# Up projection of the second block's first feed-forward by seven half products instead of eight, inner features in four portions

## What is computed

```python
def conv_ffn(h, w_up, w_conv, b_conv, w_down):
    u = dwconv_centred(h @ w_up, w_conv, b_conv)
    g, v = jnp.split(u, 2, axis=-1)
    return (jax.nn.silu(g) * v) @ w_down
```

## Time and profile before

| | |
|---|---|
| median of 3 runs | 2653.69 us (2653.25 to 2664.85) |
| profiled execution, span | 2649.1 us |
| TensorE busy | 2552.1 us |
| VectorE busy | 1718.7 us |
| ScalarE busy | 1056.5 us |
| GpSimd busy | 24.3 us |

### The profile page before, as it was taken

How to read it: one execution, slowest core, us unless ns; L and a number is a source line. 1 busy time by engine, 2 the same in 40 slices (tenths; PEclk the granted TensorE clock), 3 DMA queues, 4 the chain that set the end, 5 groups by cost and what they waited for, 6 DMA issues and landing times.

```text
span 2649.1 us, 32136 instructions
## 1 busy us (share of the span) xinstructions
PE 2552.1 (96%) x13096; PEld 2130.9 (80%) x13096; DVE 1718.7 (65%) x2364; ACT 1056.5 (40%) x1455; POOL 24.3 (1%) x31
## 2 busy tenths in 40 slices
PE   7998999999999999999989999999999999999998
PEld 6887788888778888777768888888888787788887
DVE  6886798887688877768534655235534686663563
ACT  4546442233454245443442433123324564442342
POOL 0000000000100000000000000000000000000000
PEclk9999999999899999999999999999999999999999
DMA  8432388654145666211102122211211111233232
GB/s 287 168 120 75 99 291 299 214 187 143 53 135 192 207 197 222 84 61 47 62 9 64 49 64 65 71 56 64 73 63 56 56 45 44 80 97 103 96 97 87
DMA packets 90658, 296.69 MB, mean 112 GB/s; under 512 B 9216, under 2 KB 23168, under 8 KB 90256
## 3 DMA queue, kind: packets, MB, share of 16 engines
q1 hardware_dynamic: 90512, 294.64, 34.1%
HBM read 289.88 MB, written 2.10 MB: 110 GB/s over the span
## 4 chain that ended last, share of the span: by engine, by line
PE 85%; DVE 9%; ACT 3%; issue 2%; DMA 1%; SPq 0%; DVEq 0%; ACTq 0%
PE ps L372 69%; PE ps L400 3%; PE ps L3534 1%; PE ps L3209 1%; PE ps L974 1%; PE ps L3177 1%; DVE gatt L1003 1%; DMA spare<-in_ada_w 1%; PE ps L3190 1%; PE ps L2556 1%; DVE w_lo L353 1%; PE ps L590 1%; PE ps L1981 1%; ACT w_hi L345 0%; DVE spare L504 0%
## 5 line engine op out<-in xcount | busy, mean ns | idle before, releaser
L372 PE MATMUL ps<-h_hi,w_hi 128*128 128x512 f32 (+1 forms) x2344 | 784.4, 371 | 9.4 <-DVE w_lo L353 6.4
L372 PE MATMUL ps<-h_lo,w_hi 128*128 128x512 f32 (+1 forms) x2344 | 775.2, 367 | 0.0
L372 PE MATMUL ps<-h_hi,w_lo 128*128 128x512 f32 (+1 forms) x2344 | 774.9, 367 | 0.0
L353 DVE TENSOR_TENSOR w_lo<-w_raw,w_hi 128x1024 fp32r<-128x1024 f32 (+2 forms) x318 | 412.3, 1297 | 429.4 <-ACT w_hi L345 428.4
L345 ACT ACTIVATE w_hi<-w_raw 128x1024 fp32r<-128x1024 f32 (+2 forms) x318 | 355.2, 1117 | 737.2 <-PE ps L372 686.1
L372 PEld LDWEIGHTS ps<-h_hi,w_hi 128*128 128x128 f32 x2344 | 440.6, 189 | 90.6 <-DVE w_lo L353 11.0
L372 PEld LDWEIGHTS ps<-h_hi,w_lo 128*128 128x128 f32 x2344 | 442.4, 189 | 73.9
L372 PEld LDWEIGHTS ps<-h_lo,w_hi 128*128 128x128 f32 x2344 | 442.6, 189 | 72.9 <-issue 1.4
L372 PE MATMUL ps<-g_hi,w_hi 128*128 128x512 f32 (+1 forms) x880 | 295.7, 369 | 0.8 <-DVE w_lo L353 0.8
L372 PE MATMUL ps<-g_hi,w_lo 128*128 128x512 f32 (+1 forms) x880 | 294.8, 368 | 0.0
L372 PE MATMUL ps<-g_lo,w_hi 128*128 128x512 f32 (+1 forms) x880 | 294.8, 368 | 0.0
(11 more groups left out here) (460 smaller groups left out, 2705.9 us busy)
## 6 DMA issues: line engine op xcount, KB each, us to landing
...
```

The source lines that it names most:

```text
L353: dve.tensor_tensor(low, raw_weights(k, g), high.bitcast(F32), ALU.subtract).then_inc(*k.tick("w_lo", g))
L372: last = pe.matmul(k.ps[:, product_bank(g, bank) if place is None else place, 0:tn], a[:, c, :], b[:, c, t0:t0 + tn], start=c == 0 and n = ...
```

## The change

The up projection of a pair of tiles (u and v of group j, called A11 A12 over A21 A22 with the halves of the 1024 inputs as columns) times the input (B11 B12 over B21 B22: input halves as rows, token halves 0..383 and 384..767 as columns) is eight half products of 4 slices by 384 tokens. From the third group on the kernel forms it by Winograd's variant of Strassen's seven, m = 0 to 6 in the order of `SEVEN`: A11.B11, S1.T1, S2.T2, A12.B21, S3.T3, S4.B22, A22.T4. The two first groups stay as they were (`PLAIN`).

- GpSimd makes the T sums from the whole input (for even slices it first adds `h_hi` and `h_lo` to the whole value, `pool_whole`), in place, 4 sums of 384 columns for each of 4 slices (`pool_turned`), and for each group the four weight sums S1 to S4, 512 columns each (`pool_weight_sums`). Both inputs of all these lie in SBUF. The T sums are then split by ScalarE and VectorE; T1's parts replace a half of `h_hi` and `h_lo`, so they wait for the last plain tile's product.
- A weight operand is 512 columns; each of the seven is split by itself ("split 0" to "split 6") into a ring of three buffers.
- TensorE adds products up in three banks a group: m = 0, 2, 4 and 6 in the first one, 1 and 5 in the second, 3 in the third. ScalarE copies out the intermediate states (`first_kept`, `second_kept`, `fifth_kept`, `last_kept`) before the next product of the bank, and VectorE adds in place of a copy where two terms meet ("eleven" after m = 3, "twenty_two" after m = 4, "twelve" after m = 5). m = 2 waits for `first_kept`, 4 for `second_kept`, 5 for `fifth_kept` and 6 for `twenty_two`.
- Taps and centre now read the joined values from SBUF (`source7`), not from PSUM. The taps of group j run in the time of group j+1, between its splits.
- The 22 groups go in four portions of 6, 6, 6 and 4, each followed by 8 down tiles of 6, 6, 6 or 4 slices, every one added to `x`. Of the first two down tiles of a portion the last slice is held back behind the other slices of both.
- SyncE loads four pieces of 256 KB per group (`sp_quads`), into places inside the weight buffers, instead of two tiles of 512 KB.

```diff
     run("out2", "out2", 0, KD)
-    ffn(1, 0)
+    run(("up", 1, 0, 0), "up10", 0, 2 * PLAIN)
+    for n, (first, end) in enumerate(PORTIONS):
+        run(("down", 1, 0, n), f"down10_{n}", 0, KD, end - first)
     run("qkv", "qkv", 8, 4)
     order.extend(("qkv", i, KD) for i in range(8))
     run("attout", "attout", 0, KD)
...
+def pool_seven(k):
+    for f in (0, 2, 4, 5, 6, 7):
+        if rms_direct(TALL, f):
+            pool_whole(k, f)
+        if f >= 4:
+            pool_turned(k, f - 4)
+    for j in range(PLAIN, FT):
+        pool_weight_sums(k, j)
...
+def pool_whole(k, f):
+    pool = k.nc.gpsimd
+    for bank in range(2):
+        pool.wait_ge(*k.seen("h_lo", rms_part(1, f, bank)))
+    pool.tensor_tensor(whole7(k, f), k.h_hi[:, f, :].bitcast(F32), k.h_lo[:, f, :].bitcast(F32), ALU.add).then_inc(*k.tick("pool_sum", ("whole", f)))
...
+def pool_turned(k, c):
+    pool, upper, lower = k.nc.gpsimd, whole7(k, c), whole7(k, c + 4)
+    for f in (c, c + 4):
+        pool.wait_ge(*(k.seen("pool_sum", ("whole", f)) if rms_direct(TALL, f) else k.seen("h_lo", (("rms", 1), f))))
+    step = lambda n: k.tick("pool_sum", ("turned", c, n))
+    pool.tensor_tensor(upper[:, EARLY], upper[:, LATE], upper[:, EARLY], ALU.subtract).then_inc(*step(1))
+    pool.wait_ge(*k.seen("pool_sum", ("turned", c, 1)))
+    pool.tensor_tensor(upper[:, LATE], lower[:, LATE], upper[:, LATE], ALU.subtract).then_inc(*step(3))
+    pool.wait_ge(*k.seen("pool_sum", ("turned", c, 3)))
+    pool.tensor_tensor(lower[:, LATE], lower[:, LATE], upper[:, EARLY], ALU.subtract).then_inc(*step(2))
+    pool.wait_ge(*k.seen("pool_sum", ("turned", c, 2)))
+    pool.tensor_tensor(lower[:, EARLY], lower[:, EARLY], lower[:, LATE], ALU.subtract).then_inc(*step(4))
...
+def pool_weight_sums(k, j):
+    pool, quads, (first, second) = k.nc.gpsimd, k.quads7[j % 2], (s[:, :] for s in k.sums7)
+    step = lambda n: k.tick("pool_sum", ("weights", j, n))
+    loaded = lambda name: k.seen(*quad_load(j, name))
+    a11, a12, a21, a22 = (quads[name][:, :] for name in ("A11", "A12", "A21", "A22"))
+    if j > PLAIN:
+        pool.wait_ge(*k.seen("w_lo", ("seven", j - 1, 4)))
+    else:
+        pool.wait_ge(*k.seen("product", plain_tile_before(j)))
+    pool.wait_ge(*loaded("A21"))
+    pool.wait_ge(*loaded("A22"))
+    pool.tensor_tensor(first, a21, a22, ALU.add).then_inc(*step(1))
+    if j > PLAIN:
+        pool.wait_ge(*k.seen("w_lo", ("seven", j - 1, 5)))
+    pool.wait_ge(*loaded("A11"))
+    pool.wait_ge(*k.seen("pool_sum", ("weights", j, 1)))
+    pool.tensor_tensor(second, first, a11, ALU.subtract).then_inc(*step(2))
+    pool.wait_ge(*k.seen("w_lo", ("seven", j, 1)))
+    pool.wait_ge(*k.seen("pool_sum", ("weights", j, 2)))
+    pool.tensor_tensor(first, a11, a21, ALU.subtract).then_inc(*step(3))
+    pool.wait_ge(*k.seen("w_lo", ("seven", j, 2)))
+    pool.wait_ge(*loaded("A12"))
+    pool.tensor_tensor(second, a12, second, ALU.subtract).then_inc(*step(4))
...
+def act_split7(k, j, m):
+    act, name = k.nc.scalar, SEVEN[m][0]
+    act.wait_ge(*(k.seen(*quad_load(j, name)) if name[0] == "A" else k.seen("pool_sum", ("weights", j, int(name[1])))))
+    if before7(j, m) is not None:
+        act.wait_ge(*k.seen("product", ("seven", *before7(j, m))))
+    act.activation(k.s7_hi[ring7(j, m)][:, :], weight7(k, j, m), ACT.Copy).then_inc(*k.tick("w_hi", ("seven", j, m)))
...
+def pe_seven_product(k, j, m):
+    pe, (_, operand, role), slot = k.nc.tensor, SEVEN[m], ring7(j, m)
+    pe.wait_ge(*k.seen("w_lo", ("seven", j, m)))
+    before = {0: ("kept", "last_kept"), 1: ("taken", "twelve"), 3: ("taken", "eleven")}
+    if m in before and j - 2 >= PLAIN:
+        pe.wait_ge(*k.seen(before[m][0], (before[m][1], j - 2)))
+    if m in before and j == portion_start(j) + 1:
+        pe.wait_ge(*k.seen("taken", plain_tile_before(j)))
+    if m in (2, 4, 5, 6):
+        name, what = {2: ("kept", "first_kept"), 4: ("kept", "second_kept"), 5: ("kept", "fifth_kept"), 6: ("taken", "twenty_two")}[m]
+        pe.wait_ge(*k.seen(name, (what, j)))
+    for c in range(KD // 2):
+        if j == PLAIN and operand[0] == "T":
+            pe.wait_ge(*k.seen("h_lo", ("turned", c, "first" if operand == "T1" else "rest")))
+        th, tl = operand7(k, operand, c)
+        wh, wl = (w[slot][:, c * P:(c + 1) * P] for w in (k.s7_hi, k.s7_lo))
+        for n, (a, b) in enumerate(((wh, th), (wh, tl), (wl, th))):
+            last = pe.matmul(k.ps[:, bank7(j, role), 0:HALF_T], a, b, start=m in before and c == 0 and n == 0, stop=c == KD // 2 - 1 and n == 2,
+                             skip_group_check=True)
+    last.then_inc(*k.tick("product", ("seven", j, m)))
...
+def pe_seven(k):
+    pe_pair(k, SEVEN_FIRST, TALL, k.h_hi, k.h_lo, rms_parts(1), apart=True)
+    for n in range(2, 2 * PLAIN):
+        pe_product(k, SEVEN_FIRST + n, TALL, k.h_hi, k.h_lo)
+    for n, (first, end) in enumerate(PORTIONS):
+        for j in range(max(first, PLAIN), end):
+            for m in range(len(SEVEN)):
+                pe_seven_product(k, j, m)
+        down, last, (some, whole) = BASE[DOWN, 1, 0, n], end - first - 1, down_ready(n)
+        k.nc.tensor.wait_ge(*k.seen("taken", ("twelve", end - 1)))
+        for i in range(2):
+            pe_product(k, down + i, TALL, k.g7_hi, k.g7_lo, [some], part=range(last))
+        for i in range(2):
+            pe_product(k, down + i, TALL, k.g7_hi, k.g7_lo, [None] * last + [whole], part=range(last, last + 1))
+        for i in range(2, KD):
+            pe_product(k, down + i, TALL, k.g7_hi, k.g7_lo)
+    pe_sums(k, ("rms", 2))
...
+def dve_joined(k, j, name):
+    dve = k.nc.vector
+    m, role, part, tokens, kept = {"eleven": (3, 2, 0, EARLY, "first_kept"), "twenty_two": (4, 0, 1, LATE, "fifth_kept"),
+                                   "twelve": (5, 1, 0, LATE, "second_kept")}[name]
+    c = k.c7[part][:, tokens]
+    dve.wait_ge(*k.seen("product", ("seven", j, m)))
+    dve.wait_ge(*k.seen("kept", (kept, j)))
+    dve.tensor_tensor(c, k.ps[:, bank7(j, role), 0:HALF_T], c, ALU.add).then_inc(*k.tick("taken", (name, j)))
...
+def act_centre7(k, j, part):
+    act, (taps, bias) = k.nc.scalar, ffn_taps(k, 1, 0, 0, j, part)
+    if j < PLAIN:
+        act.wait_ge(*k.seen("product", SEVEN_FIRST + 2 * j + part))
+    elif part == 0:
+        act.wait_ge(*k.seen("taken", ("twelve", j)))
+    else:
+        act.wait_ge(*k.seen("taken", ("twenty_two", j)))
+        act.wait_ge(*k.seen("kept", ("last_kept", j)))
...
+def act_seven_pair(k, j, down):
+    behind = j - 1 >= PORTIONS[portion_of(j)][0]
+    act_split7(k, j, 2)
+    if behind:
+        if j - 1 >= PLAIN:
+            act_last_kept(k, j - 1)
+        act_centre7(k, j - 1, 1)
+    act_first_kept(k, j)
+    if behind and j - 1 >= PLAIN:
+        act_silu7(k, j - 1)
+    act_split7(k, j, 3)
+    act_split7(k, j, 4)
+    act_second_kept(k, j)
+    act_fifth_kept(k, j)
+    act_split7(k, j, 5)
+    if behind:
+        act_g_high7(k, j - 1)
+    act_split7(k, j, 6)
+    if down is not None:
+        k.nc.scalar.wait_ge(*k.seen("w_lo", ("seven", j, len(SEVEN) - 1)))
+        act_split(k, down)
+    else:
+        act_split7(k, j + 1, 0)
+    act_centre7(k, j, 0)
+    if down is not None:
+        act_split(k, down + 1)
+    else:
+        act_split7(k, j + 1, 1)
...
+def dve_seven_pair(k, j, down):
+    behind = j - 1 >= PORTIONS[portion_of(j)][0]
+    dve_split7(k, j, 2)
+    if behind and j - 1 >= PLAIN:
+        dve_tap7(k, j - 1, 0, 2)
+    dve_split7(k, j, 3)
+    if behind:
+        dve_tap7(k, j - 1, 1, 1)
+    dve_split7(k, j, 4)
+    if behind:
+        dve_tap7(k, j - 1, 1, 2)
+    dve_split7(k, j, 5)
+    if behind:
+        dve_gated7(k, j - 1)
+    dve_split7(k, j, 6)
+    dve_joined(k, j, "eleven")
+    if behind:
+        dve_g_low7(k, j - 1)
+    dve_joined(k, j, "twenty_two")
+    if down is not None:
+        dve_split(k, down)
+    else:
+        dve_split7(k, j + 1, 0)
+    dve_joined(k, j, "twelve")
+    if down is not None:
+        dve_split(k, down + 1)
+    else:
+        dve_split7(k, j + 1, 1)
+    dve_tap7(k, j, 0, 1)
```

More of the change, by code:

```diff
@@ L36 @@
 LATS = slice(CTX, TALL)
+HALF_T = TALL // 2
 WIDE = 2
@@ new lines, in sp_seven @@
+def sp_seven(k):
+    sp = k.nc.sync
+    sp_fetch(k, SEVEN_FIRST + 3)
+    for n, (first, end) in enumerate(PORTIONS):
+        start, down = max(first, PLAIN), BASE[DOWN, 1, 0, n]
+        if n == 0:
+            sp_quads(k, start)
+            sp_quads(k, start + 1)
+        for j in range(start + 2, end):
+            sp_quads(k, j)
+        sp.wait_ge(*k.seen("w_lo", ("seven", end - 2, len(SEVEN) - 1)))
+        for i in range(KD):
+            sp_fetch(k, down + i)
+        if n + 1 < len(PORTIONS):
+            sp_quads(k, end)
+            sp_quads(k, end + 1)
+    for i in range(3):
+        sp_fetch(k, QKV + i)
@@ new lines, in act_centre7 @@
+def act_centre7(k, j, part):
+    act, (taps, bias) = k.nc.scalar, ffn_taps(k, 1, 0, 0, j, part)
+    if j < PLAIN:
```

(16 more changed lines are left out.)

251 lines of the change are left out of this document (237 added, 14 removed).

## The result

The changed kernel takes **2737.8 us** (median of 4 runs, 2736.9 to 2740.2), against 2659.1 of the kernel before on the same chip: 1.031 times as long, with a 95% interval of 1.028 to 1.034. The forecast was slower, 2695, with a range up to 2724: the sign is right, the size is half. On the profiled spans it is 2735.9 against 2649.1, +86.8 us where the sum had +41.5.

A forecast was written before the change was run, and what follows sets the result against it. The prediction took a VectorE-ScalarE loop of 18.0 us a pair as the bound. Terms 26.8 + 6.4 + 2.6 + 5.7 gave +41.5 on 2649.1, 2690.6; with 4.6 for the median, 2695 us, range 2654 to 2724.

The forecast's parts named there:

- the sum: Whole span: extra time of rewritten pairs, borders to the down tiles and beginning added together, +41.5 us on 2649.1.
- The bound: Rewritten up pairs: hand-overs between VectorE and ScalarE set the pace at 18.0 us a pair, not TensorE's 14.7.
- The three waits named: Rewritten pairs: TensorE waits for first_kept at product 2, split 5 at product 5 and twenty_two at product 6.
- the loop of 18.0: Steady pair, from "twelve" to the next: eight alternating VectorE and ScalarE parts with eight hand-overs, 18.0 us.
- GpSimd's holds: Weight sums in a steady pair: S3 alone delays VectorE, by 0.84 us; S4, S1 and S2 fall in gaps.
- Portions: Up tiles of a portion of n pairs: first pair 14.7 us, each later one the steady period; +26.8 us in all.
- P: Time of a steady rewritten pair: 18.0 plus one GpSimd delay of 0.84, 18.8 us.
- Beginning: Before the first rewritten pair: released splits, GpSimd delays in the normalisation and a late last T, +5.7 us, from 1.7 to 15.
- Borders: Up to down tiles: TensorE waits 1.9 us three times and near 0.7 once, +6.4; short last portion +2.6.
- A: Rival for the steady pair: GpSimd finds only idle time, 18.0 us a pair, 2678 us; chance 0.16.
- C: Rival for the steady pair: more or longer GpSimd delays, 20.4 us a pair, 2721 us; chance 0.16 together with D.
- D: Rival: TensorE's clock drops; at 0.75 the pair takes 19.6 us, 2708 us; chance 0.16 together with C.

The follow-up runs named there:

- the version of 2636.4 us: Changed kernel with both ScalarE's and VectorE's queues reordered within a pair and the four weight sums moved from GpSimd to VectorE: 2636.4 us, ratio 0.993.
- the late start: Against a reordered kernel with weight sums on VectorE (2632.0 us): GpSimd begins T sums only after the normalisation's last h_lo, splits reordered; 2635.1 us, ratio 0.992.

## Why the prediction was half right

- **The bound** (loop, not TensorE): right. 18.00 measured without GpSimd's sums, 18.0 forecast. TensorE's 14.7 a pair: 14.75. The three waits named are there: `first_kept` and `twenty_two` in all 16 steady pairs, the one on split 5 (L3242) with just under 1.0 us in eight of them. But the prediction named them for the loop of 18.0, and in the run with that loop only the one on `twenty_two` is over 0.3 us; the other two come with the holds.
- **GpSimd's holds: the step that failed.** The prediction gave S4, S1 and S2 no cost, since their turn would come in gaps. S2's did, S4's and S1's did not: the count was one, it is three. The size was taken as 0.84, it is 1.04. Two holds too few are 2.08 a pair and 0.2 belong to the size: 21.08 against 18.8, over the 16 pairs (the last of each portion 20.0 to 20.3) 33.2 us, the larger part of the 45.3 that the sum is short. The rest is 4.4 in the first rewritten pair, 6.0 before it, 3.7 at the down tiles, less 2.0 outside. The count came from "GpSimd lets two or so pass"; of the operations run here only scalings by two columns do that. Had S4 and S1 been given their turn behind the running piece, both would have fallen on a second tap and the text would have had three holds.
- The size lies between the ends that the prediction took (0.42 and 1.54), near their middle (0.98); the estimate of 1.12 from the Trainium skill (GPSIMD Engine Reference, "Elementwise — side-by-side cycle accounting") is nearer than 0.84, partly by luck: a sum alone takes 1.26 us here, longer than that estimate, and what VectorE loses is 1.04, less than all of it. With 1.12 and a count of one the pair would still have been 19.1.
- **Portions**: "14.7 + (n-1) P" holds. With the measured periods, what is left for the first pair is 15.5, 14.4 and 14.7 in the second to fourth portion, but 19.1 in the first: 4.4 us of the beginning lie there. Some 1.5 of them are TensorE's clock: the first nine matmuls of the pair start 0.32 us apart and more (half clock from 1505.8 to 1509.2) instead of 0.17. Another 1.4 is the wait that the list puts down to "issue": its seventh product starts at 1521.77, when `twenty_two` has ended (1521.67).
- **Beginning**: +11.7 and these 4.4 make 16, forecast 5.7 with a bound of 15 (its own three upper ends, 1.7, 6.3 and 8, add up to 16): mis-sized. The normalisation loses 5.6 (forecast 3). The clock isn't the reason, though it was 0.82 there and 0.92 before: the version of 2636.4 us with GpSimd as early has 0.94 and takes the same 28.40 us, and the late start takes 23.75 at 0.93. The wait for split 0, 5.4, had no term: the two splits of the "rest" of T stand before it in both queues, ScalarE's behind the silu of group 1, and GpSimd holds two of VectorE's instructions there. With the weight sums on VectorE it is 3.1 to 3.3.
- **Borders**: right. 2.1 three times, 0.8 and 2.1, against 1.9, 0.7 and 2.6, all in the places named. The down tiles took some 3.6 us more beside these waits (12.7 less 9.2). About 2 us of it are matmuls that start farther apart, 24 of them in 4.24 us instead of 4.16 in most of the first and last portion's tiles; why is open.
- **Rivals**: A (the sums take nothing) is out: 21.08 with them, 18.00 without. C had the right sign (more holds) with P = 20.4 and still fell short by 0.7, as it kept one of the holds out. Its reason was the reverse of what happened: S4 and S1 missed their gaps since their turn came early, not late. D is out as the cause. Its observation isn't: stretches at 1.2 GHz do appear in the pair (granted clock 0.92), inside TensorE's idle share. They also are why TensorE is busy 79% of the pair (16.62 of 21.08), next to the 78% forecast: the agreement is luck, as both numbers of the forecast, 14.7 and 18.8, were lower.
